# The second block's last convolution channel tile: diagonal f32 matmuls on TensorE in place of taps on VectorE, ScalarE and GpSimd

## The chip, the cores and the metric

The kernel runs on one core of one Trainium2 chip. The metric is the device time of one launch in microseconds: 1757.15 us, median of three runs (1757.03 to 1757.19).

## The reference, cut to what matters

Two transformer blocks follow each other over 512 tokens with model width 1024, all in float32. The second block has, beside an RWKV-7 recurrence of 8 heads, a convolution branch of 512 channels: a gated input, a causal depthwise convolution of 31 taps, a LayerNorm over the channels, and SiLU.

```python
def conformer_conv(u, conv_w, conv_b, ln_g, ln_b):
    h = u[..., :D_CONV] * jax.nn.sigmoid(u[..., D_CONV:])
    h = lax.conv_general_dilated(
        h, conv_w[:, None, :], window_strides=(1,), padding=[(CONV_WIDTH - 1, 0)],
        dimension_numbers=("NWC", "WIO", "NWC"), feature_group_count=D_CONV) + conv_b
    h = layer_norm(h, ln_g, ln_b)
    return jax.nn.silu(h)
...
    y_conv = conformer_conv(p[..., :2 * D_CONV], ...)
    y_rwkv, v_first = rwkv7_mix(p[..., 2 * D_CONV:], ...)
    y = jnp.concatenate([y_conv, y_rwkv], axis=-1) @ w_out[i]
```

Depthwise means that channel c of the result is the sum over the 31 taps of conv_w[tap, c] times channel c of the input, shifted by the tap. Both branches must be there before the product with w_out.

## The kernel before, in words

Activations lie with channels on the 128 partitions and the 512 tokens along the free dimension, so the 512 convolution channels are four tiles, ZC[0] to ZC[3], each 128x542 with 30 leading zeros. A tap of a tile is one pass over 128x512 elements of it at offset `tap`, scaled by a column of weights.

One function, `schedule()`, writes down a single list of steps for all engines, and each engine then emits its own part of every step in that order (`run`). All engines are in-order: an instruction that waits holds back what stands behind it on its engine. Background work is held in Python generators; each call of `pl.step` lets every generator put a few steps. Generators stand in the order conv (`cv1`), conv on GpSimd (`cv2`), `prep` (gates, scan and scaling of a pair of heads `hp`), four `head` generators (the inverse of the recurrence of a head, in levels of 64x64 matmuls), `fin` (states and outputs of a pair). The last projection tile of the block marks `pdone`, and from there `pl.drain()` runs the generators in rounds. I call these rounds R1, R2 and so on. In a round the convolution generators put two steps (weight 2) and each of the others one. A head's round alternates between `x` (a mask product, its transposition, and one more product) and `z` (an update), and every such product is evicted from PSUM by VectorE or ScalarE before the next round's matmuls can start.

The four tiles are shared out like this:
- Tiles 1 and 2: 31 taps each on VectorE (`tap_v`), accumulating in a PSUM bank (`conv.acc`).
- Tile 0: for taps 1 to 30 ScalarE multiplies into one of two buffers, F(45) and F(46) (`tap_g` of ScalarE), and GpSimd adds that to the sum (`tap_g` of GpSimd). ScalarE waits before tap t until GpSimd has done tap t - 2.
- Tile 3: taps 5 to 30 (CSH = 26 of them) in the same ScalarE and GpSimd way into CP = F(58), taps 0 to 4 on VectorE after tile 2, and `conv.join` adds the two parts.

GpSimd reaches tile 3 while the projection tiles 11 to 13 are still running (its first instruction for it is at 976.95 us of the trace) and adds its last tap in R11. VectorE's taps of tile 2 fill two places in each of R1 to R13, with R1's pair at 999.23 us, and tile 3's five taps stand in R14 (two), R15 (two) and R16 (one, with the join after it). The statistics and the norm of the convolution follow from R17 on. `bg_out`, the product of the convolution branch with w_out, starts in R23.

PSUM has 8 banks. In the rounds 6 are in pool M, handed out first in, first out; a step that takes a bank makes TensorE wait until the former user of that bank has been evicted. Through R1 to R13 `conv.acc` of tile 2 holds one of the 6, so 5 go round; in R14 to R16 `conv.acc` of tile 3 holds one.

In each round the steps stand in this order: the convolution's taps, then prep's step for pair hp, then the heads' steps, then fin's. R3 holds `prep.kn` of pair 2, R4 its `prep.vmm`, R6 its `prep.scale`, R7 its `prep.shift`, R8 its `prep.turn`; R11, R12, R13, R14 and R15 hold the scan, `prep.norm`, `prep.kn`, `prep.vmm` with `prep.scale`, and `prep.shift` of pair 3. A pair's chain ends at R10 to R12 with `fin.mu` (R9), `fin.var`, `fin.rs`, `fin.g`.

All matmuls go through the helper `Eng.mm` (line 153), ScalarE copies through `Eng.cp` (L162) and `Eng.act` (L159), elementwise VectorE and GpSimd operations through `Eng.tt` (L165), `Eng.ts` (L169/L170) and `Eng.stt` (L173). So the rows of the profile show helper lines, and an operation is told by its form. One f32 `mm` call leaves two MATMUL instructions in the trace; a call on the float32r operands of the dense layers leaves one.

Of the kernel before, what the change touches and what calls it, by code (L numbers as in the profile page):

```python
# [8 lines left out]
CSH = 26  # L9
LAST = {1: 30, 2: 30, 3: 30 - CSH}  # L10
# [168 lines left out]
class Plan:  # L179
# [13 lines left out]
    def put(self, *step):  # L193
        self.steps.append(step)
# [19 lines left out]
    def has(self, *keys):  # L214
        return all(k in self.done for k in keys)
# [90 lines left out]
def schedule():  # L306
# [242 lines left out]
    def bg_conv_pool():  # L549
        yield from taps(0, 0, 31, "g")  # L550
        yield from taps(3, 31 - CSH, 31, "g")
        mark("cp")

    def bg_conv():
        for i in range(1, 4):
            while not has(("hc", i)):
                yield
            pl.take("M", "conv.acc", i)
            for tap in range(LAST[i] + 1):
                while tap == LAST[i] and i > 1 and not has(("pdone",)):  # L560
                    yield
                put("tap.v", i, tap)
                yield
            pl.rel("M", "conv.acc", i)
        while not has(("cp",)):
            yield
        put("conv.join")
        yield
        pl.take("M", "conv.mean")
        put("conv.mean")  # L570
        pl.rel("M", "conv.mean")
        yield
        for i in range(4):
            put("conv.sq", i)
            yield
        pl.cols("conv.n", "M")
        yield
        pl.spread("conv.n", "M")
        yield
        for i in range(5):  # L580
            if i < 4:
                put("conv.scale", i)
            if i > 0:
                put("conv.out", i - 1)
            yield
        mark("conv")

    cv1, cv2 = bg_conv(), bg_conv_pool()
    pl.begin(cv1, cv2)
    pl.pace[cv1], pl.pace[cv2] = 4, 3  # L590
    pl.weight[cv1], pl.weight[cv2] = 2, 2
# [399 lines left out]
def program(nc, wstream, vecs, cf, cu, xT, metaT, memT, pmix, gup, wau, gupg, out, x2s, kvs):  # L991
# [5 lines left out]
    with ctx:  # L997
# [90 lines left out]
        def freed(*key):  # L1088
            k = pl.before[key]
            if k and k[0] in ("fin.y1", "fin.yc"):  # L1090
                return k[0:2]
            if k and k[0] in DIRECT:
                return DIRECT[k[0]]
            if k and k[0] == "xr.t":
                return ("xr.s", k[1][0:2], 7, 1)
            return k
# [41 lines left out]
        CO, CP = [F(i) for i in CS], F(58)  # L1138
# [163 lines left out]
        def tensor(e):  # L1302
# [171 lines left out]

            def conv_mean():
# [220 lines left out]
            def att_out(g, d):  # L1696
# [10 lines left out]
                "gla.state": gla_state, "gla.out": gla_out, "mix": mix, "conv.mean": conv_mean,  # L1707
# [10 lines left out]
        def scalar(e):  # L1718
# [158 lines left out]
            def tap_g(i, tap, t0):  # L1877
                if tap > t0:
                    wc = vcol("conv_w_2") + tap * 4 + i
                    before = ("conv.g", i, tap - 2) if tap - 2 > t0 else ("conv.g", 0, 30 - tap % 2) if i else None  # L1880
                    e.wait_ge(("mid.hc", i), before)
                    e.cp(F(45 + tap % 2), ZC[i][:, tap:tap + 512], scale=V[:, wc:wc + 1]).then_inc(*e.up("conv.m", i, tap))

# [168 lines left out]
            def evh_dn(i, h):  # L2052
# [8 lines left out]
                "ev.f1": ev_f1, "ev.f2": ev_f2, "ev.cv": ev_cv, "tap.g": tap_g, "conv.sq": conv_sq,  # L2061
# [10 lines left out]
        def vector(e):  # L2072
# [229 lines left out]
            def conv_join():  # L2302
                e.wait_ge(("conv.acc", 3), ("conv.g", 3, 30))
                e.tt(CO[3], CO[3], CP, ADD).then_inc(*e.up("conv.j"))
# [286 lines left out]
        def gpsimd(e):  # L2591
# [53 lines left out]
            def tap_g(i, tap, t0):  # L2645
                dst = CP if i else CO[0]
                c = vcol("conv_w_2") + tap * 4 + i
                if tap == t0:
                    src, w_ = ZC[i][:, tap:tap + 512], V[:, c:c + 1]
                    e.wait_ge(("mid.hc", i))  # L2650
                    if i:
                        e.ts(dst, src, w_, MUL).then_inc(*e.up("conv.g", i, tap))
                    else:
                        e.ts(dst, src, w_, MUL, s2=vec("conv_b_2", i), o2=ADD).then_inc(*e.up("conv.g", i, tap))
# [245 lines left out]
```

## Time and profile before

| what | value |
|---|---|
| median of 3 runs | 1757.15 us |
| the profiled execution's own time | 1757.04 us |
| its span, first to last instruction | 1755.1 us |
| mean granted TensorE clock | 0.968 |
| PE busy | 1661.0 us (95%) |
| VectorE (DVE) busy | 838.8 us (48%) |
| ScalarE (ACT) busy | 606.0 us (35%) |
| GpSimd (POOL) busy | 389.4 us (22%) |

The table is over the whole span. The rounds of the second block's recurrence, roughly 997 to 1140 us, look different from the rest: there TensorE has gaps, its granted clock drops at times, and VectorE is nearly always busy. Times in the rows are microseconds from the span's start. PE is TensorE's matmul side, PEld its weight loads. In a timeline the bracket behind a row is the idle time of that engine before it and the engine and line that ended it.

### The profile page before, as it was taken

How to read it: one execution, taken by the hardware profiler on the slowest of the kernel's cores; microseconds unless marked ns; L12 is line 12 of the kernel's file. 1: busy time of each engine (PE TensorE's matmuls, PEld its weight loads, DVE VectorE, ACT ScalarE, POOL GpSimd, SP SyncE). 2: the span in 40 equal slices, each digit the busy share in tenths (PEclk: the TensorE clock that was granted, in tenths of full speed). 3: DMA queues.
4: the chain of work that ended last, by engine and by line, in shares of the span. 5: the costliest groups of instructions: out<-in, count | busy, mean ns of one | idle time of the engine just before them, and what ended most of it. 6: DMA issues, size and time to landing. Idle time of an engine off the chain costs nothing.

```text
span 1755.1 us, 26846 instructions
## 1 busy us (share of the span) xinstructions
PE 1661.0 (95%) x11510; PEld 1365.6 (78%) x11510; DVE 838.8 (48%) x1256; ACT 606.0 (35%) x973; POOL 389.4 (22%) x333
## 2 busy tenths in 40 slices
PE   6999999999999999999998877898999999999997
PEld 5789878787888888888776666777878878888876
DVE  3377642435433333344756887645642632333334
ACT  4143432324323232243335442334334432222222
POOL 2112111212201011133034540103102341131133
PEclk8899999999999999999999889999999999999999
DMA  5123421224222223222411100013211222223222
GB/s 195 61 84 121 145 73 49 76 87 150 97 96 94 98 76 108 80 96 84 144 50 49 49 3 3 3 50 108 109 41 56 97 88 105 75 94 103 89 78 66
DMA packets 29829, 146.03 MB, mean 83 GB/s; under 512 B 4096, under 2 KB 7440, under 8 KB 14608
## 3 DMA queue, kind: packets, MB, share of 16 engines
q1 hardware_dynamic: 29712, 144.33, 23.4%
q8 instruction: 91, 1.49, 0.4%
q14 instruction: 26, 0.21, 0.0%
HBM read 138.03 MB, written 6.29 MB: 82 GB/s over the span
## 4 chain that ended last, share of the span: by engine, by line
PE 77%; DVE 8%; issue 7%; POOL 4%; ACT 3%; DMA 1%; POOLq 0%; SPq 0%; DVEq 0%; ACTq 0%
PE ps L153 76%; POOL zf L165 3%; DVE zf L165 3%; DVE zf L173 2%; DVE wl L165 1%; DVE ps L173 1%; ACT zf L159 1%; ACT zf L162 1%; ACT wh L162 1%; DMA raw<-in_wstream 1%; ACT zr L162 1%; POOL tn L165 1%; PE ps L156 1%; DVE zf L2344 0%; DVE zr L173 0%
## 5 line engine op out<-in xcount | busy, mean ns | idle before, releaser
L153 PE MATMUL ps<-zr,wh 128*128 128x512 f32 (+1 forms) x3936 | 1173.7, 383 | 16.2 <-DVE wl L165 9.9
L153 PEld LDWEIGHTS ps<-zr,wh 128*128 128x128 f32 x3936 | 716.6, 190 | 175.2 <-DVE wl L165 9.8
L153 PE MATMUL ps<-zr,wl 128*128 128x512 f32 (+1 forms) x1968 | 745.7, 379 | 0.0
L165 POOL TENSOR_TENSOR zf<-zf 128x512 f32<-128x512 f32 (+1 forms) x237 | 283.5, 1203 | 856.4 <-ACT zf L159 587.5
L153 PEld LDWEIGHTS ps<-zr,wl 128*128 128x128 f32 x1968 | 374.0, 190 | 77.1 <-issue 0.8
L165 DVE TENSOR_TENSOR wl<-raw,wh 128x1024 fp32r<-128x1024 f32 (+1 forms) x243 | 306.2, 1300 | 230.5 <-ACT wh L162 230.3
L162 ACT ACTIVATE wh<-raw 128x1024 fp32r<-128x1024 f32 (+1 forms) x243 | 240.4, 1038 | 213.6 <-PE ps L153 211.8
L159 ACT ACTIVATE zf<-zf 128x512 f32<-128x512 f32 (+2 forms) x232 | 127.5, 561 | 396.3 <-DVE zf L165 282.2
L153 PE MATMUL ps<-zf 64*64 64x64 f32 (+6 forms) x3640 | 203.3, 248 | 32.3 <-DVE zf L165 18.1
L153 PEld LDWEIGHTS ps<-zf 64*64 64x64 f32 (+3 forms) x3640 | 162.7, 150 | 72.7 <-issue 31.1
L165 DVE TENSOR_TENSOR zf<-ps,zf 128x512 f32<-128x512 f32 (+2 forms) x165 | 97.6, 597 | 202.8 <-PE ps L153 176.0
L162 ACT ACTIVATE zf<-ps 128x512 f32<-128x512 f32 (+2 forms) x160 | 74.3, 483 | 185.3 <-PE ps L153 169.9
L165 POOL TENSOR_TENSOR zr<-zf,zr 128x512 fp32r<-128x512 f32 x54 | 70.1, 1300 | 280.3 <-ACT zr L162 280.3
L165 DVE TENSOR_TENSOR zf<-zf,ps 128x512 f32<-128x512 f32 (+1 forms) x112 | 62.6, 570 | 140.8 <-PE ps L153 139.7
L162 ACT ACTIVATE zr<-zf 128x512 fp32r<-128x512 f32 x74 | 46.5, 632 | 168.2 <-POOL zf L165 140.0
L153 PE MATMUL ps<-cf_sb,zf 64*64 64x64 f32 (+2 forms) x988 | 64.0, 237 | 24.4 <-ACT zf L159 11.6
L153 PEld LDWEIGHTS ps<-cf_sb,zf 64*64 64x64 f32 (+1 forms) x988 | 59.7, 159 | 28.9 <-POOL zf L165 10.2
L165 POOL TENSOR_TENSOR tn<-tn,cf_sb 128x2 f32<-128x2 f32 (+3 forms) x29 | 31.5, 1089 | 207.3 <-DVE tn L169 115.4
L173 DVE SCALAR_TENSOR_TENSOR zf<-ps,zf 128x512 f32<-128x512 f32 x46 | 31.4, 690 | 92.6 <-PE ps L153 88.6
L162 ACT ACTIVATE zf<-zf,vecs_sb 128x512 f32<-128x512 f32 x73 | 49.7, 716 | 44.2 <-DVE zf L165 36.5
L173 DVE SCALAR_TENSOR_TENSOR ps<-zf,vecs_sb,ps 128x512 f32<-128x512 f32 (+1 forms) x93 | 61.2, 658 | 5.0 <-PE ps L153 3.9
L173 DVE SCALAR_TENSOR_TENSOR zr<-zf,vecs_sb,zr 128x256 fp32r<-128x256 f32 (+1 forms) x64 | 43.8, 696 | 33.0 <-ACT zr L162 33.0
(94 smaller groups left out, 713.1 us busy)
## 6 DMA issues: line engine op xcount, KB each, us to landing
raw<-in_wstream SPq DMA_DIRECT2D x117, 1024.0 KB, 4.8
zf<-in_xT SPq DMA_DIRECT2D x16, 256.0 KB, 3.1
raw<-in_wstream SPq DMA_DIRECT2D x4, 768.0 KB, 4.3
kv_scratch<-zf SPq DMA_DIRECT2D x8, 256.0 KB, 2.2
x_scratch<-zf SPq DMA_DIRECT2D x8, 256.0 KB, 2.1
zf<-x_scratch SPq DMA_DIRECT2D x8, 256.0 KB, 4.4
out<-zf SPq DMA_DIRECT2D x16, 128.0 KB, 1.7
zf<-in_cu SPq DMA_DIRECT2D x1, 1256.0 KB, 10.1
```

The source lines that it names most:

```text
L153: return self.raw.matmul(out_, l, x, start=start, stop=stop)
L156: return self.raw.transpose(out_, in_, idn)
L159: return self.raw.activation(out_, in_, fn, bias=bias, scale=scale)
L162: return self.raw.activation(out_, in_, mybir.ActivationFunctionType.Copy, scale=scale)
L165: return self.raw.tensor_tensor(out_, a, b, o)
L173: return self.raw.scalar_tensor_tensor(out=out_, in0=a, scalar=s, in1=b, op0=o1, op1=o2)
```

## The change

Tile 3 leaves VectorE, ScalarE's multiplications and GpSimd. For each of its 31 taps ScalarE scales the 128x128 identity by the tap's weight column into one of four buffers (CD, which lie in F(58), the former CP), and TensorE multiplies that diagonal matrix with ZC[3] at the tap's offset, 128x128 by 128x512 in f32, accumulating all 31 in one PSUM bank, `conv.p`. A third generator puts these steps two in each round from R1 on (R1 to R15 two, R16 one), before prep, heads and fin. It takes the bank in R1 and gives it back with the join. ScalarE's build of tap t waits for the matmul of tap t - 4. `conv.join` becomes one VectorE operation: PSUM plus the bias into CO[3]. GpSimd keeps tile 0, and the wait that let its second tile follow its first is gone. The join moves from the second place of R16 to the first of R17 and `conv.mean` stays in R17.

```diff
@@ -6,8 +6,7 @@
 P = 128
 UNIT = 2048
 DECAY = math.exp(-0.5)
-CSH = 26
-LAST = {1: 30, 2: 30, 3: 30 - CSH}
+LAST = {1: 30, 2: 30}
 PFIRST = 3
 LAG = 1
 
@@ -548,11 +547,19 @@
 
     def bg_conv_pool():
         yield from taps(0, 0, 31, "g")
-        yield from taps(3, 31 - CSH, 31, "g")
         mark("cp")
 
+    def bg_conv_pe():
+        while not has(("hc", 3), ("pdone",)):
+            yield
+        pl.take("M", "conv.p")
+        for tap in range(31):
+            put("tap.p", tap)
+            yield
+        mark("cpe")
+
     def bg_conv():
-        for i in range(1, 4):
+        for i in range(1, 3):
             while not has(("hc", i)):
                 yield
             pl.take("M", "conv.acc", i)
@@ -562,9 +569,10 @@
                 put("tap.v", i, tap)
                 yield
             pl.rel("M", "conv.acc", i)
-        while not has(("cp",)):
+        while not has(("cp",), ("cpe",)):
             yield
         put("conv.join")
+        pl.rel("M", "conv.p")
         yield
         pl.take("M", "conv.mean")
         put("conv.mean")
@@ -585,10 +593,11 @@
             yield
         mark("conv")
 
-    cv1, cv2 = bg_conv(), bg_conv_pool()
-    pl.begin(cv1, cv2)
+    cv1, cv2, cv3 = bg_conv(), bg_conv_pool(), bg_conv_pe()
+    pl.begin(cv1, cv2, cv3)
     pl.pace[cv1], pl.pace[cv2] = 4, 3
-    pl.weight[cv1], pl.weight[cv2] = 2, 2
+    for g in (cv1, cv2, cv3):
+        pl.weight[g] = 2
     pl.rate = 2
 
     def lag():
@@ -1091,6 +1100,8 @@
                 return k[0:2]
             if k and k[0] in DIRECT:
                 return DIRECT[k[0]]
+            if k and k[0] == "conv.p":
+                return ("conv.j",)
             if k and k[0] == "xr.t":
                 return ("xr.s", k[1][0:2], 7, 1)
             return k
@@ -1135,7 +1146,9 @@
         SC = [F(62 + z) for z in range(4)]
         ZC = [ZF[:, 47 * 512 + 542 * i:47 * 512 + 542 * (i + 1)] for i in range(4)]
         CS = [64, 44, 22, 23]
-        CO, CP = [F(i) for i in CS], F(58)
+        CO = [F(i) for i in CS]
+
+        CD = [F(58)[:, 128 * i:128 * i + 128] for i in range(4)]
         ZB = [F(42), F(43)]
         wau_sb, gupg_sb = F(40), F(41)
         km_ap = [F(47 + i // 2)[:, (i % 2) * 256:(i % 2) * 256 + 256] for i in range(8)]
@@ -1472,6 +1485,11 @@
                 e.wait_ge(freed("in.mx", g), ("in.pool", g), ("in.pm",))
                 e.mm(ps("in.mx", g)[:, :], pmx[:, g * 128:(g + 1) * 128], F(43 + g)).then_inc(*e.up("mm", "in.mx", g))
 
+            def tap_p(tap):
+                e.wait_ge(freed("conv.p") if tap == 0 else None, ("mid.hc", 3), ("conv.d", tap))
+                e.mm(ps("conv.p")[:, :], CD[tap % 4], ZC[3][:, tap:tap + 512], start=(tap == 0),
+                     stop=(tap == 30)).then_inc(*e.up("mm", "conv.p", tap))
+
             def conv_mean():
                 b = ps("conv.mean")
                 e.wait_ge(freed("conv.mean"), ("conv.g", 0, 30), ("conv.acc", 1), ("conv.acc", 2), ("conv.j",))
@@ -1704,7 +1722,7 @@
             run(e, {
                 "mm": mm, "mmm": mmm, "kt": kt, "ko": ko, "mh": mh, "koh": koh, "rows": rows, "cols": cols, "spread": spread, "gla.gate": gla_gate,
                 "gla.score": gla_score, "gla.turn": gla_turn, "gla.turnm": gla_turnm, "gla.state0": gla_state0,
-                "gla.state": gla_state, "gla.out": gla_out, "mix": mix, "conv.mean": conv_mean,
+                "gla.state": gla_state, "gla.out": gla_out, "mix": mix, "tap.p": tap_p, "conv.mean": conv_mean,
                 "prep.gates": prep_gates, "prep.norm": prep_norm, "prep.kn": prep_kn, "prep.vmm": prep_vmm,
                 "prep.turn": prep_turn, "head.a": head_a, "head.pk": head_pk, "head.rt": head_rt, "head.qt": head_qt,
                 "head.ta": head_ta, "head.tz": head_tz, "head.x": head_x, "head.z": head_z, "head.px": head_px,
@@ -1877,9 +1895,13 @@
             def tap_g(i, tap, t0):
                 if tap > t0:
                     wc = vcol("conv_w_2") + tap * 4 + i
-                    before = ("conv.g", i, tap - 2) if tap - 2 > t0 else ("conv.g", 0, 30 - tap % 2) if i else None
-                    e.wait_ge(("mid.hc", i), before)
+                    e.wait_ge(("mid.hc", i), ("conv.g", i, tap - 2) if tap - 2 > t0 else None)
                     e.cp(F(45 + tap % 2), ZC[i][:, tap:tap + 512], scale=V[:, wc:wc + 1]).then_inc(*e.up("conv.m", i, tap))
+
+            def tap_p(tap):
+                c = vcol("conv_w_2") + tap * 4 + 3
+                e.wait_ge(("mm", "conv.p", tap - 4) if tap >= 4 else ("ffn.h", 31))
+                e.cp(CD[tap % 4], ident, scale=V[:, c:c + 1]).then_inc(*e.up("conv.d", tap))
 
             def conv_sq(i):
                 e.wait_ge(("conv.mean",) if i == 3 else ("conv.mt", i))
@@ -2058,7 +2080,7 @@
                 "gla.log": gla_log, "gla.exp": gla_exp, "gla.ends": gla_ends, "gla.turn": gla_turn,
                 "gla.turnm": gla_turnm, "gla.state0": gla_state0, "gla.out": gla_out, "gla.sq": gla_sq, "mix": mix,
                 "ev.po": ev_po, "ev.r": ev_r, "ev.ga": ev_ga, "ev.gb": ev_gb, "og": og, "ev.go": ev_go, "ev.wo": ev_wo,
-                "ev.f1": ev_f1, "ev.f2": ev_f2, "ev.cv": ev_cv, "tap.g": tap_g, "conv.sq": conv_sq,
+                "ev.f1": ev_f1, "ev.f2": ev_f2, "ev.cv": ev_cv, "tap.g": tap_g, "tap.p": tap_p, "conv.sq": conv_sq,
                 "conv.scale": conv_scale, "ev.p": ev_p, "p.mix": p_mix, "prep.gates": prep_gates,
                 "prep.decay": prep_decay, "prep.kk": prep_kk, "prep.v": prep_v, "prep.scale": prep_scale, "prep.shift": prep_shift,
                 "prep.turn": prep_turn, "head.ta": head_ta, "head.tz": head_tz, "head.px": head_px, "head.gh": head_gh,
@@ -2300,8 +2322,8 @@
                     e.stt(CO[i], src, w_, acc, MUL, ADD).then_inc(*e.up("conv.acc", i))
 
             def conv_join():
-                e.wait_ge(("conv.acc", 3), ("conv.g", 3, 30))
-                e.tt(CO[3], CO[3], CP, ADD).then_inc(*e.up("conv.j"))
+                e.wait_ge(("mm", "conv.p", 30), ("mm", "t.p", 13))
+                e.ts(CO[3], ps("conv.p")[:, :], vec("conv_b_2", 3), ADD).then_inc(*e.up("conv.j"))
 
             def conv_mean():
                 e.wait_ge(("mm", "conv.mean"))
@@ -2643,15 +2665,12 @@
                 power(tn_of("mid.b"), ("mid.b3",), "mid.b2")
 
             def tap_g(i, tap, t0):
-                dst = CP if i else CO[0]
+                dst = CO[0]
                 c = vcol("conv_w_2") + tap * 4 + i
                 if tap == t0:
                     src, w_ = ZC[i][:, tap:tap + 512], V[:, c:c + 1]
                     e.wait_ge(("mid.hc", i))
-                    if i:
-                        e.ts(dst, src, w_, MUL).then_inc(*e.up("conv.g", i, tap))
-                    else:
-                        e.ts(dst, src, w_, MUL, s2=vec("conv_b_2", i), o2=ADD).then_inc(*e.up("conv.g", i, tap))
+                    e.ts(dst, src, w_, MUL, s2=vec("conv_b_2", i), o2=ADD).then_inc(*e.up("conv.g", i, tap))
                 else:
                     e.wait_ge(("conv.m", i, tap), ("conv.g", i, tap - 1))
                     e.tt(dst, dst, F(45 + tap % 2), ADD).then_inc(*e.up("conv.g", i, tap))
```

## Rows read from the trace of the kernel before

**Rows 1.** The page: shares of the chain that ended last, over the whole span.
```profile
PE 77%; DVE 8%; issue 7%; POOL 4%; ACT 3%; DMA 1%; POOLq 0%; SPq 0%; DVEq 0%; ACTq 0%
```

**Rows 2.** Busy time by stretch: per engine us and (instructions), then PEclk, DMA share, GB/s.
```profile
997.20:1011.10 13.90, 9.61 (x164) 9.29 (x165) 12.12 (x24) 5.43 (x10) 8.61 (x7) 0.51 0.01 2
...
1031.60:1038.40 6.80, 2.87 (x54) 2.90 (x56) 6.25 (x9) 0.74 (x2) 2.76 (x2) 0.50 0.02 4
...
1069.20:1092.00 22.80, 18.18 (x486) 16.66 (x488) 16.23 (x34) 5.71 (x13) 0.00 (x0) 0.85 0.01 3
```

**Rows 3.** Timeline of TensorE in the rounds: the rows behind its gaps.
```profile
997.22 2.83 PE L153 MATMUL ps<-zf 64*64 64x64 f32 x60 [2.66 <-ACT zf L159]
1004.32 1.54 PE L153 MATMUL ps<-zf 64*64 64x64 f32 x24 [4.26 <-DVE zf L165]
...
1020.32 1.12 PE L153 MATMUL ps<-zf,cf_sb 128*128 128x512 f32 x2 [3.41 <-DVE zf L165]
...
1035.53 1.12 PE L153 MATMUL ps<-zf 64*64 64x64 f32 x16 [7.02 <-DVE zf L165]
...
1048.18 1.12 PE L153 MATMUL ps<-zf,cf_sb 128*128 128x512 f32 x2 [0.93 <-DVE zf L165]
...
1059.54 0.68 PE L153 MATMUL ps<-cf_sb,zf 64*64 64x64 f32 x16 [1.78 <-DVE zf L165]
...
1069.33 1.97 PE L153 MATMUL ps<-cf_sb,tn 128*64 128x128 f32 x16 [3.30 <-POOL tn L165]
...
1085.71 2.65 PE L153 MATMUL ps<-zf 64*64 64x64 f32 x83 [2.86 <-DVE zf L165]
```

**Rows 4.** Timeline of VectorE in the rounds.
```profile
997.54 1.76 DVE L173 SCALAR_TENSOR_TENSOR zf<-zf,vecs_sb 128x511 f32<-128x511 f32 x1
...
1000.67 2.25 DVE L2344 TENSOR_TENSOR_SCAN zf<-cu_sb,zf 128x512 f32<-128x512 uint8 x1
...
1004.30 0.88 DVE L165 TENSOR_TENSOR zf<-zf,cu_sb 128x256 f32<-128x256 f32 x2
...
1018.29 1.64 DVE L173 SCALAR_TENSOR_TENSOR zf<-zf,vecs_sb 128x512 f32<-128x512 f32 x1
...
1029.96 3.42 DVE L173 SCALAR_TENSOR_TENSOR zf<-zf 128x512 f32<-128x512 f32 x2
1033.42 1.63 DVE L165 TENSOR_TENSOR zf<-zf 128x512 f32<-128x512 f32 x1
...
1056.93 1.22 DVE L2344 TENSOR_TENSOR_SCAN zf<-cu_sb,zf 128x512 f32<-128x512 uint8 x1
...
1073.19 0.75 DVE L173 SCALAR_TENSOR_TENSOR zf<-zf,vecs_sb 128x512 f32<-128x512 f32 x1
...
1083.09 1.41 DVE L173 SCALAR_TENSOR_TENSOR zf<-zf 128x512 f32<-128x512 f32 x2
1084.54 0.69 DVE L165 TENSOR_TENSOR zf<-zf 128x512 f32<-128x512 f32 x1
...
1087.85 1.54 DVE L173 SCALAR_TENSOR_TENSOR ps<-zf,vecs_sb,ps 128x512 f32<-128x512 f32 x2
```

**Rows 5.** Timeline of ScalarE just before R1.
```profile
993.32 1.94 ACT L162 ACTIVATE zf<-zf,vecs_sb 128x512 f32<-128x512 f32 x3
995.87 0.72 ACT L162 ACTIVATE zf<-zf,vecs_sb 128x512 f32<-128x512 f32 x1 [0.61 <-POOL zf L165]
996.50 1.25 ACT L159 ACTIVATE zf<-ps,vecs_sb 128x512 f32<-128x512 f32 x2
```

**Rows 6.** Groups of GpSimd, 976 to 1048 us: busy us, mean ns, idle before.
```profile
L165 POOL TENSOR_TENSOR zf<-zf 128x512 f32<-128x512 f32 x26 | 36.4, 1400 | 31.4 <-ACT zf L162 28.8
```

**Rows 7.** Timeline of TensorE: the four f32 calls of the convolution's mean.
```profile
1095.15 3.70 PE L153 MATMUL ps<-zf,cf_sb 128*128 128x512 f32 x8
```

**Rows 8.** Groups of ScalarE, 990 to 1100 us.
```profile
L162 ACT ACTIVATE zf<-zf,vecs_sb 128x512 f32<-128x512 f32 x27 | 18.5, 717 | 6.8 <-POOL zf L165 3.6 <-DVE zf L165 3.0
...
L159 ACT ACTIVATE dsm<-dsm 128x8 f32<-128x8 f32 x2 | 0.4, 208 | 8.6 <-DVE dsm L165 8.6
```

## The prediction, made before the changed kernel ran

> **What bounds the kernel now.** I read the chain of waits first. Over the span TensorE holds 77% of it [rows 1], so most of the kernel is dense matmuls that this change does not touch. The change lies in R1 to R16, from 997.2 to about 1092 us, and there the picture is another one. By stretches [rows 2] TensorE is busy 9.61 of the first 13.90 us and VectorE 12.12; between 1031.6 and 1038.4 TensorE has 2.87 of 6.80 and VectorE 6.25. The third thing to see in those rows is the clock: 0.51 and 0.50 in two of the stretches and 0.85 in the third, so TensorE spends part of this stage at 1.2 GHz, and each time it had been idle before.
>
> The timeline of TensorE [rows 3] then gives each gap and who ended it: 2.66 us for ScalarE, 4.26, 3.41, 7.02, 1.78 and 2.86 us for VectorE, 3.30 us for GpSimd's power that stands between `prep.norm` and `prep.kn` of pair 3. So the rounds are a ring of TensorE and VectorE. A round is as long as its matmuls plus the evictions behind them, and where prep has much elementwise work, VectorE alone sets it. The taps of the convolution are filler in this ring, but filler that stands ahead of the heads' steps in every queue.
>
> **The change, part by part.** I sum against the profiled execution's 1757.04 us (span 1755.1, 1.94 us outside it), which is 0.11 us under the median of the runs.
>
> *ScalarE's hold before R1 goes.* ScalarE does three tap products (1.94 us), waits 0.61 us for GpSimd's sum, does a fourth (0.72), and only then the two tanh of the gates of pair 2 at 996.50 [rows 5]. TensorE waits for these: 2.66 us [rows 3]. The products and the wait, 3.27 us, are gone before the tanh (the diagonals are not put until R1), so the whole gap closes: -2.7.
>
> *VectorE stops being slowed by GpSimd.* GpSimd's adds for tile 3 take most of the 36.4 us of [rows 6], and they lie on 976.95 to 1047 us. In that time some VectorE operations take far longer than the same form later, when GpSimd is idle [rows 4]: the scan of prep 2.25 against 1.22; the STT of two SBUF tiles 1.64 against 0.75; two of them in `prep.scale` 3.42 against 1.41, and the multiplication after them 1.63 against 0.69; and the mix of the last projection tile 1.76, against which I set the 0.75 of the STT one element longer. A tap into PSUM (1.54 the pair) has that price in R15, with GpSimd idle, and in the rounds before as well. What I expect: 1.01 and 1.03 in R1, 0.89 twice in R3 (the second such operation of `prep.kn` stands right before the one shown, alike), 2.01 and 0.94 in R6. In R1 not all of this is won, see the bank below. R3 -1.8, R6 -2.95. The other end is 0, if the stretching has another cause.
>
> *VectorE loses five taps and the join changes form.* Five at 0.75 to 0.8. The two of R15 (1.54) and the one of R16 (0.75) stand between a state update and `prep.shift` or the last masks, with TensorE waiting: -2.2 of 2.3. The pair of R14 stands beside TensorE's transposition of v and costs nothing. The join is one 128x512 operation in both kernels: 0.
>
> *TensorE gets 31 f32 matmuls.* Before, the four f32 calls of the mean, the same shape and accumulating in one bank, took 3.70 us [rows 7], 0.925 each. 31 make 28.7 us, 1.85 in each of R1 to R15. The Trainium skill ("FP8 and Floating Point Precision", TensorE Precision Notes) counts four passes for true f32; at 2.4 GHz that is 0.85 us for 512 columns and 26.5 us for 31, an estimate; the row is 8% above it and is what I use. What of it lies on the path, by round:
> - R1: the pair runs while VectorE is still at scan and masks (gap of 4.26): 0.
> - R2: TensorE is done with the small `prep.norm` matmuls 1.4 us before VectorE has done its own taps: 0.4. R4: the gap of 3.41 shrinks by R3's 1.8 to 1.6, so 1.85 leaves 0.2.
> - R6 and R7: the gap of 7.02 less 2.95 is 4.1, and two pairs are 3.7: 0. R12 and R13: the gap of 3.30 and the time until VectorE reads `prep.norm`: 0. R15: the gap of 2.86: 0.
> - R3, R5, R8, R9, R10, R11, R14 and half of R16: nothing but small gaps stands there, so 7.5 pairs, 13.9 us, less the gaps of 0.93 and 1.78: 11.2.
>
> Together +11.8. The bounds: 0, if all is hidden, and 28.7, if none is (at the low clock twice that again for the pairs that meet it).
>
> *ScalarE's 31 diagonals.* 128x128 with a weight column is not in the trace. Below is the 128x8 activation, 208 ns, above the 128x512 of the same form, 717 ns [rows 8]. The size is nearer to the small one, so I take 300 ns: 0.6 a round, where two tap products of 0.7 were until R10. The builds stand behind ScalarE's evictions of the round before, which TensorE's heads need anyway. Cost 0. If it doesn't hold, see the fourth case.
>
> *One bank less.* In R1 to R13 `conv.p` and `conv.acc` both hold banks, so 4 go round in place of 5. In R1 the last `fin.n` product takes the bank of the second head's mask and not of the first's. That is evicted one product, one addition and one mask later: 0.88 us for the first two [rows 4] and near half of that for the mask, 1.3, its place being the gap of 4.26. It eats that much of the 2.04 of R1 and leaves -0.7. In R9 `fin.mu` waits for one eviction more in the same way (its gap of 0.93 is for this): +1.2. Elsewhere the evictions are ahead. In R14 to R16 nothing changes, as `conv.acc` of tile 3 is not taken. Bounds 0 and 5 (0.4 more in the x rounds too).
>
> *The clock.* About 22 us of matmul work in the rounds runs at 1.2 GHz (9.6, 2.9 and, from the third stretch's 0.85, near 6.8 [rows 2], the rest around 1022). At 2.4 GHz it would take 11 us less. The spells come with the gaps, and the taps and the quicker VectorE fill most of those; but some of that work is evictions rather than columns, and R1 keeps a gap. I take half: -5.5, between 0 and -11. The Trainium skill ("TensorE: Matmul & The Clock Gate", What's actually happening) has activity release the throttle. By that rule, with the gaps of R4, R7, R13 and R15 filled, nearly all spells vanish, which is the second case.
>
> *The tail.* The join comes one place later, but `conv.mean` stays in R17, and by counting places `bg_out` still starts in R23: 0.
>
> Sum: -2.7 -0.7 -1.8 -2.95 -2.2 +11.8 +1.2 -5.5 = -2.85. ScalarE's evictions in the x rounds also find a shorter queue (0.6 in place of 1.4 us [rows 8]); I give that 0.5, so -3.35. 1757.0 - 3.3 = 1753.7.
>
> **The rivals.**
> 1. *Likeliest, 0.45*: as summed, 1753.7, own range 1751 to 1756.5.
> 2. *The clock holds, 0.20*: the full 11 us in place of 5.5, 1748.2. For it: every low stretch has a gap in or before it. Against it: R1's gap stays, and a spell may just move.
> 3. *The clock gives nothing, 0.20*: the spells move with the stage, 1753.7 + 5.5 = 1759.2. For it: even the stretch from 1069 us, with GpSimd idle, has 0.85. Against it: 28.7 us of wide matmuls are the strongest filling there is.
> 4. *The diagonals come late, 0.15*: TensorE's pair waits behind ScalarE's evictions of the round before and then for the build, an eviction of 0.4 and two builds of 0.6, so 1.0 in each of 7.5 bare rounds, +7.5: 1761.2, slower than before. Place: TensorE's wait for ScalarE ahead of the first tap of a round. It decides as soon as ScalarE reaches the builds later than TensorE ends the last round. For it: the buffers are built in the round of their use, not ahead. Against it: in the z rounds ScalarE has nothing to evict, and it is the least busy of the three.
>
> **How the numbers follow.** About 3.5 us, 0.2%, is what a measurement of this kernel can tell from no change. Faster by more, under 1753.6: half of case 1 and all of case 2, and a little of 3: 0.46. Within: the rest of case 1, most of 3, a third of 4: 0.38. Slower, over 1760.7: the rest of 4, and case 3 where the bank costs its upper bound: 0.16. The range goes from 1746.5 (case 2 with a little more of the taps hidden) to 1761.5 (just past case 4).
>
> **What would show it.** GpSimd idle from about 975 us to the powers of pair 2, no 2.66 us gap before R1, the scan of pair 2 at 1.2 us and `prep.scale`'s pair at 1.4: the gains in R1 to R6. TensorE's tap pair 1.85 us apart in the timeline, the gaps at R4, R7, R13 and R15 nearly closed, PEclk above 0.85 from 997 to 1092: the filling and the clock. R16's end earlier by 3 to 4 us than before, then the same lengths until the end. It would be wrong if TensorE waits for ScalarE's diagonals, if the VectorE operations stay long with GpSimd idle, or if R8 to R11 grow by more than 1.85 each.

## The result, and the profile after

Slower. The median is 1774.63 us (1773.36 to 1787.05, four runs) against 1757.17 us for the kernel before on the same chip, +17.5 us; the ratio is 1.0114, 95% interval 1.0069 to 1.0159. The forecast of 1753.7 us is missed by 21 us and its range by 13. The profiled execution took 1774.54 us (span 1772.6).

The kernels share their frame up to the rounds, and `conv.mean`, where the change ends, comes 17.0 us later (1095.15 in [rows 7], 1112.11 now). So all of the loss lies between R1 and there. In the page the chain that ended last is nearly what it was [rows 1]:

```profile
PE 78%; DVE 8%; issue 7%; POOL 4%; ACT 3%; DMA 1%; POOLq 0%; SPq 0%; DVEq 0%; ACTq 0%
```

Shares of the whole span cannot show this loss, since 17 us in 1770 are 1%. I use two stretches, cut where the work is the same in every kernel: from VectorE's tap pair of R1 to that of R13 (R1 to R12), and from there to `conv.mean` (R13 to R17). Columns as in [rows 2]: window, its length, then busy us and (instructions) of PE, PEld, DVE, ACT and POOL, PEclk, DMA share, GB/s. Before:

```profile
999.23:1068.71 69.48, 48.51 (x1138) 43.39 (x1134) 58.68 (x113) 27.46 (x55) 29.04 (x21) 0.84 0.01 2
1068.71:1095.15 26.44, 21.32 (x547) 19.50 (x547) 18.82 (x40) 7.67 (x17) 0.48 (x1) 0.87 0.01 3
```

The kernel after, the same two, and R2 alone:

```profile
996.75:1078.38 81.63, 70.36 (x1262) 49.95 (x1262) 53.83 (x114) 24.15 (x62) 4.93 (x3) 0.96 0.01 2
1078.38:1112.11 33.73, 26.12 (x560) 19.18 (x559) 16.14 (x36) 9.33 (x22) 0.00 (x0) 0.95 0.01 2
1004.16:1013.54 9.38, 9.04 (x208) 6.83 (x206) 3.48 (x10) 1.84 (x6) 1.65 (x1) 0.80 0.01 2
```

R1 to R12 grew by 12.2 us and R13 to R17 by 7.3, although VectorE has less to do and the clock rose from 0.84 and 0.87 to 0.96 and 0.95. Outside TensorE's busy time there are 18.9 us in place of 26.1. (Some records of small matmuls are missing from the trace of the kernel before: R1 to R12 show 1138 there, and 1262 less the 48 of the taps, so 1214, in the kernel after. So the kernel before has somewhat more busy time and less idle time than these figures say; the lengths of the stretches don't depend on it.)

What the change was meant to do to the other engines did happen. ScalarE just before R1, which answers to [rows 5]: the tap products are gone, the gates' evictions come 2.1 us earlier, and two diagonals stand behind them. (One product of the same form is left, at 993.76. The kernel without tile 3's products has it too, at 993.54, so it is no tap, and one of the four that the prediction counted in [rows 5] was never part of the hold.)

```profile
993.76 0.72 ACT L161 ACTIVATE zf<-zf,vecs_sb 128x512 f32<-128x512 f32 x1 [1.37 <-DVE zf L164]
994.39 1.25 ACT L158 ACTIVATE zf<-ps,vecs_sb 128x512 f32<-128x512 f32 x2
995.53 0.69 ACT L161 ACTIVATE zf<-cf_sb,vecs_sb 128x128 f32<-128x128 f32 x2
```

The operations of VectorE in [rows 4] that were long have their short durations, 0.74 for 1.76, 1.22 for 2.25, 0.75 for 1.64, 1.41 for 3.42, 0.69 for 1.63:

```profile
995.75 0.42 DVE L169 TENSOR_SCALAR zf<-zf 128x512 f32<-128x512 f32 x1
996.09 0.74 DVE L172 SCALAR_TENSOR_TENSOR zf<-zf,vecs_sb 128x511 f32<-128x511 f32 x1
...
998.20 1.22 DVE L2366 TENSOR_TENSOR_SCAN zf<-cu_sb,zf 128x512 f32<-128x512 uint8 x1
...
1019.14 0.75 DVE L172 SCALAR_TENSOR_TENSOR zf<-zf,vecs_sb 128x512 f32<-128x512 f32 x1
...
1032.42 1.41 DVE L172 SCALAR_TENSOR_TENSOR zf<-zf 128x512 f32<-128x512 f32 x2
1033.87 0.69 DVE L164 TENSOR_TENSOR zf<-zf 128x512 f32<-128x512 f32 x1
```

The first of these rows is VectorE's first operation behind ScalarE's gates. In the kernel before it was

```profile
997.20 0.43 DVE L170 TENSOR_SCALAR zf<-zf 128x512 f32<-128x512 f32 x1 [1.03 <-ACT zf L159]
```

so it comes 1.45 us earlier now, and the mix behind it (0.74 for 1.76) adds 1.0 us before VectorE's tap pair of R1.

On GpSimd, 976 to 1048 us, the 36.4 us of [rows 6] have become one addition:

```profile
L164 POOL TENSOR_TENSOR zf<-zf 128x512 f32<-128x512 f32 x1 | 1.6, 1554 | 0.1
```

TensorE's timeline shows where new time stands; its gaps answer to [rows 3], the last row to [rows 7]:

```profile
996.07 3.33 PE L152 MATMUL ps<-zf 128*128 128x512 f32 x64 [2.41 <-ACT zf L161]
1000.81 6.51 PE L152 MATMUL ps<-zf 64*64 64x64 f32 x60 [1.42 <-DVE zf L164]
...
1014.23 1.99 PE L152 MATMUL ps<-zf 128*128 128x512 f32 x4 [0.93 <-ACT zf L161]
...
1054.61 3.59 PE L152 MATMUL ps<-zf 128*128 128x512 f32 x21 [1.47 <-ACT zf L161]
...
1112.11 3.67 PE L152 MATMUL ps<-zf,cf_sb 128*128 128x512 f32 x8 [1.35 <-DVE zf L168]
```

The gap before R1 is still there (2.41 for 2.66): the first tap pair waits for its diagonals. The gap of 4.26 in R1 is 1.42. A pair of taps takes 1.99 us. In the waits of TensorE from 994 to 1092 us (us in all, times, longest) ScalarE's copies, the diagonals among them (L161), stand first, and VectorE's 21.9 us are 6.5:

```profile
PE ps L152 <- ACT zf L161: 8.8, 7, 2.4
PE ps L152 <- DVE zf L164: 6.5, 6, 2.0
```

ScalarE's 31 builds cost 394 ns each, against which [rows 8] had 717 for a product and 208 for a small activation (group over 990 to 1115 us: busy, mean ns, idle before):

```profile
L161 ACT ACTIVATE zf<-cf_sb,vecs_sb 128x128 f32<-128x128 f32 x31 | 10.5, 394 | 0.0
```

L161 is the helper of all copies; where diagonals are built early (an experiment below), 0.8 us of such waits remain, so about 8 of the 8.8 are the diagonals'. Read alone, these rows say that rival 4 came true. The experiments show that this is not where the 17.5 us went.

### The profile page after: what moved, and what is told of

It is laid out like the page before. It is cut to its first block, busy times and chain, and to the rows that moved or that the text cites. A ratio compares the mean times of both kernels' runs of the same rounds, so it can differ in the third digit from the quotient of the medians.

```text
span 1772.6 us, 26915 instructions
## 1 busy us (share of the span) xinstructions
PE 1685.6 (95%) x11572; PEld 1370.5 (77%) x11572; DVE 829.3 (47%) x1251; ACT 599.6 (34%) x979; POOL 353.9 (20%) x307
## 4 chain that ended last, share of the span: by engine, by line
PE 78%; DVE 8%; issue 7%; POOL 4%; ACT 3%; DMA 1%; POOLq 0%; SPq 0%; DVEq 0%; ACTq 0%
PE ps L152 77%; POOL zf L164 3%; DVE zf L164 2%; DVE zf L172 2%; DVE wl L164 1%; DVE ps L172 1%; ACT zf L161 1%; ACT zf L158 1%; DMA raw<-in_wstream 1%; ACT wh L161 1%; ACT zr L161 1%; POOL tn L164 1%; PE ps L155 0%; DVE zf L2366 0%; POOL zr L164 0%
## 5 line engine op out<-in xcount | busy, mean ns | idle before, releaser
L164 POOL TENSOR_TENSOR zf<-zf 128x512 f32<-128x512 f32 (+1 forms) x212 | 249.7, 1184 | 833.6 <-ACT zf L158 598.7
L161 ACT ACTIVATE wh<-raw 128x1024 fp32r<-128x1024 f32 (+1 forms) x243 | 240.4, 1038 | 213.0 <-PE ps L152 210.5
L152 PE MATMUL ps<-zf 64*64 64x64 f32 (+6 forms) x3702 | 231.7, 250 | 29.4 <-ACT zf L161 14.9
L152 PEld LDWEIGHTS ps<-zf 64*64 64x64 f32 (+3 forms) x3702 | 169.0, 146 | 86.2 <-issue 43.7
L161 ACT ACTIVATE zf<-ps 128x512 f32<-128x512 f32 (+2 forms) x160 | 74.5, 484 | 214.8 <-PE ps L152 189.2
L161 ACT ACTIVATE zr<-zf 128x512 fp32r<-128x512 f32 x74 | 46.5, 632 | 167.4 <-POOL zf L164 140.1
L164 DVE TENSOR_TENSOR zf<-zf 128x512 f32<-128x512 f32 (+4 forms) x74 | 50.7, 699 | 11.1 <-ACT zf L158 10.7
```

Of the source, the lines that this page charges most:

```text
L152: return self.raw.matmul(out_, l, x, start=start, stop=stop)
L161: return self.raw.activation(out_, in_, mybir.ActivationFunctionType.Copy, scale=scale)
L164: return self.raw.tensor_tensor(out_, a, b, o)
```

## The experiments

Each number is a median less the median of the kernel before, measured beside it on the same chip, then the ratio with its 95% interval (0.001 of the ratio is 1.8 us). Kernels from different sections ran on different chips, so their differences to the kernel before are compared, and a difference of 1 or 2 us between two of them is not resolved. "Early" means that a diagonal is built a round before its use.

### The gains alone

The kernel before without the taps of tile 3 that ScalarE and GpSimd make (taps 5 to 30 are left out). VectorE's five and the bank of their sum stay, nothing is given to TensorE.

```
-        yield from taps(3, 31 - CSH, 31, "g")
...
-                e.wait_ge(("conv.acc", 3), ("conv.g", 3, 30))
-                e.tt(CO[3], CO[3], CP, ADD)
+                e.wait_ge(("conv.acc", 3))
+                e.ts(CO[3], CO[3], 1.0, MUL)
```

> The kernel before with tile 3's taps 5 to 30 left out on ScalarE and GpSimd (their sum is not added; taps 0 to 4 stay on VectorE). It measures the gain side of the change alone. Theory A (the gains came as predicted, the matmuls and ScalarE's diagonals cost more than they): 8 to 11 us under the kernel before, about 1747. Rival B (the gains of R1 and R6 are given back later, since the rounds hang on other waits): within 3 us of the kernel before, 1754 to 1757.

Measured: 1750.33, -7.9 us; 0.9948 (0.9933 to 0.9963). The two stretches of its trace:

```profile
996.53:1060.62 64.09, 48.79 (x1132) 43.52 (x1128) 52.39 (x113) 17.16 (x38) 4.45 (x3) 0.84 0.01 3
1060.62:1086.28 25.66, 19.58 (x546) 17.90 (x546) 18.64 (x39) 7.66 (x17) 0.48 (x1) 0.93 0.01 4
```

R1 starts 2.7 us earlier, R3 lasts 5.47 us in place of 7.30 and R6 4.95 in place of 7.92; R11 gives 1.0 back (11.37 for 10.38). Here, where no diagonal stands in the way, TensorE's gap before R1 is 0.55 us:

```profile
994.89 1.90 PE L153 MATMUL ps<-zf 64*64 64x64 f32 x60 [0.55 <-ACT zf L159]
```

The side of the gains was sized nearly right (7.9 us, just under the 8 to 11 expected). From here on the question is what costs 25 us, not 17.5.

### The matmuls taken out, and the change repeated

From the changed kernel, taps 1 to 29 have no matmul (29 of 31 taps are left out of tile 3); all 31 diagonals are built, each behind the one four before it, and the bank is held. Beside it the changed kernel again, unedited.

```
             def tap_p(tap):
+                if 0 < tap < 30:
+                    return
```

> The changed kernel with the matmuls of taps 1 to 29 left out; taps 0 and 30 stay, all 31 diagonals are built, the bank is held. Theory A (TensorE's own time is most of the loss): 1750 to 1755. Rival C (ScalarE's queue and the bank): over 1760.

> The changed kernel once more, unchanged, so that the other three have it on the same chip. 1773 to 1776 under every theory.

Measured: without matmuls 1760.70, +2.7 us; 1.0016 (1.0006 to 1.0026). The change again 1775.76, +17.8; 1.0107 (1.0090 to 1.0123). So the 29 matmuls are worth 15.1 us of their 26.8, and what is left is still 10.6 us above the kernel with the gains alone. The 15.1 are a net value: without the matmuls TensorE's clock is lower (0.81 in R1 to R12, which last 72.53 us, against 0.96 and 81.63 with them). The 10.6 are the bank, or diagonals that almost nothing waits for; the next runs part these.

### The diagonals early, or not built

First: `tap.d` for taps 0 and 1 before R1, then for tap t + 2 behind tap t. Second: matmuls with the identity in place of the diagonals and no build on ScalarE (all 31 weights of tile 3 are left out).

```
+            put("tap.d", 0)
+            put("tap.d", 1)
...
             put("tap.p", tap)
+            if tap + 2 < 31:
+                put("tap.d", tap + 2)
```
```
-                e.mm(ps("conv.p")[:, :], CD[tap % 4], ZC[3]...
+                e.mm(ps("conv.p")[:, :], ident, ZC[3]...
```

> The changed kernel with each diagonal built one round ahead: taps 0 and 1 before R1, tap t + 2 right behind the step of tap t. TensorE waited 9.6 us in all for ScalarE ahead of these matmuls. Theory D (late diagonals are a cost of their own): 7 to 10 us under the changed kernel, about 1766. Rival A2 (the wait only stands in the place of the one for VectorE or for the state update that ends the round before): under 3 us of gain, 1772 or more.

> The changed kernel with the identity in place of all 31 diagonals and ScalarE's builds left out (the sum is then unweighted). The matmuls are the same in number and form. Under theory D it goes as the kernel with early diagonals or 1 to 2 us below it, 1764 to 1766, and what is left over e1's time is TensorE's matmuls and the bank. Under rival A2 it stays at 1771 or more.

Measured: early 1769.96, +11.8; 1.0061 (1.0046 to 1.0076). Identity 1769.44, +11.2; 1.0060 (1.0041 to 1.0079). So the building itself costs nothing that can be seen if it is early enough, and lateness costs about 6 of the 17.8 us with this number of banks. That lies between the two expectations (7 to 10 us, or under 3). Two thirds of the loss are something else.

### The bank

`conv.p` from D, a pool that stands idle in the rounds, in place of M, from which the heads' steps take theirs; once with early diagonals and once as the only edit of the changed kernel.

```
-        pl.take("M", "conv.p")
+        pl.take("D", "conv.p")
...
-        pl.rel("M", "conv.p")
+        pl.rel("D", "conv.p")
```

> The kernel with early diagonals (e3_early), with the bank for the sum taken from pool D, whose two banks lie idle in R1 to R16, so 5 go round in pool M as before the change. Theory E (the missing bank costs 2 to 5 us): 1765 to 1768. Rival (it costs nothing, evictions are ahead): within 1 us of e3_early's 1770.

> The changed kernel with the sum's bank from pool D and nothing else: diagonals are built late as in the changed kernel. If bank and late diagonals add, it is 4 to 6 us above the kernel with both mended (1763.9), so 1768 to 1770. If they are one and the same wait (a late diagonal is only late because the ring of 4 banks is), it is within 2 us of 1764.

Measured: early with the bank of D 1763.85, +5.9; 1.0039 (1.0024 to 1.0054). The bank alone 1763.27, +4.9; 1.0028 (1.0019 to 1.0038). Two changed words give back 12.9 us of 17.8, and with them early diagonals bring nothing more: the bank is worth more than the 2 to 5 us expected, and the two mends don't add. Stretches of the bank alone, and its R2:

```profile
996.59:1071.53 74.94, 66.41 (x1262) 47.45 (x1262) 53.40 (x114) 23.92 (x62) 4.93 (x3) 1.00 0.01 2
1071.53:1101.06 29.53, 24.40 (x560) 18.80 (x559) 15.96 (x36) 9.44 (x22) 0.00 (x0) 1.00 0.01 2
1004.01:1009.97 5.96, 5.48 (x205) 5.18 (x203) 3.29 (x11) 1.86 (x6) 1.65 (x1) 1.00 0.01 3
```

Half of the 6.7 us that R1 to R12 lose to the bank is R2, 9.38 against 5.96 us. The number of instructions is nearly the same (208 and 205); the clock is 1.00 in place of 0.80. The low spell starts in R1, whose clock is 0.79 in the change and 1.00 here: by windows of 1 us it stands at 0.50 from 1001 to 1007 us and at 0.59 in the next, near 7 us in all. At half the clock this loses an estimated 3.4 us, and as VectorE sets the length of R1 (7.41 and 7.42 us), it shows in R2. What TensorE did before it, here:

```profile
995.91 4.09 PE L152 MATMUL ps<-zf 128*128 128x512 f32 x96 [2.40 <-ACT zf L161]
1000.66 0.92 PE L152 MATMUL ps<-zf 64*64 64x64 f32 x24 [0.66 <-DVE zf L164]
```

The gap of 0.66 was 1.42 in the change. It ends at the same moment of R1 (4.1 us after VectorE's tap pair starts, in both), but with the bank 32 more matmuls fit ahead of it. From R3 to R12 the clock is 1.00 in both kernels, so the other 3.3 us of R1 to R12 (1.3 in R4, 1.0 in R10, 0.5 each in R7 and R11) are not the clock. The kernel with early diagonals shows the same thing from the other side. Its R1 pair is done sooner, so a longer gap stands behind it:

```profile
1000.81 5.26 PE L152 MATMUL ps<-zf 64*64 64x64 f32 x28 [3.11 <-DVE zf L164]
```

and then R2 takes 9.64 us at 0.64, though it has the bank:

```profile
1004.16:1013.80 9.64, 9.64 (x208) 8.51 (x207) 3.47 (x11) 1.86 (x6) 1.65 (x1) 0.64 0.01 3
```

That is why "early" brought nothing here: what it won in R10 and R12 (7.68 and 2.85 us against 9.41 and 4.88) it lost in R2. In the kernel with late diagonals both rounds hold a wait for them; R12's is

```profile
1066.36 1.98 PE L152 MATMUL ps<-zf 128*128 128x512 f32 x4 [2.33 <-ACT zf L161]
```

The counterpart: the kernel before, from which one bank of M is taken at R1, left empty, and given back at the join.

```
+    def bg_hold():
+        while not has(("hc", 3), ("pdone",)):
+            yield
+        held.append(pl.pools["M"].pop(0))
...
         put("conv.join")
+        pl.pools["M"].append(held.pop())
```

> The kernel before with one more bank of pool M held idle from R1 to the join, so that 4 go round in R1 to R13 and 4 in R14 to R16; nothing else differs. Theory E (the bank alone is a main cost, 5 to 10 us): 1763 to 1768. Rival (my step's +1.2 and 1.3, by eviction order): 1758 to 1761.

Measured: 1771.88, +13.5; 1.0066 (1.0048 to 1.0084), by which it would be 11.6; more than the 5 to 10 expected. No tap matmul and no diagonal is in it. Its stretches:

```profile
1001.00:1081.45 80.45, 57.30 (x1154) 49.66 (x1154) 58.77 (x114) 27.79 (x55) 29.00 (x21) 0.73 0.01 2
1081.45:1109.06 27.61, 21.18 (x546) 19.22 (x546) 18.91 (x39) 7.77 (x17) 0.48 (x1) 0.88 0.01 3
```

R1 to R12 last 11.0 us longer than before. 8.8 of it is TensorE's busy time, for nearly the same instructions (1154 records and 1138), at 0.73 in place of 0.84; only 2.2 are more idle time. The largest part is R10, 9.86 us at 0.68 in place of 5.85 at 1.00. `fin.mu` shows how it begins: at the end of R9 three short gaps follow each other, and then the matmuls that took 1.12 us in [rows 3] take 2.08:

```profile
1055.18 0.68 PE L153 MATMUL ps<-zf 64*64 64x64 f32 x16 [0.88 <-DVE zf L165]
1056.43 0.68 PE L153 MATMUL ps<-cf_sb,zf 64*64 64x64 f32 x16 [0.57 <-DVE zf L165]
1057.69 2.08 PE L153 MATMUL ps<-zf,cf_sb 128*128 128x512 f32 x2 [0.57 <-DVE zf L165]
```

### Filling by gap, and fewer matmuls

24 taps on TensorE in the rounds where it has gaps (4, 0, 0, 2, 1, 2, 3, 0, 1, 0, 2, 1, 3, 1, 3, 1 in R1 to R16), seven on GpSimd after tile 0; bank of D, diagonals early.

```
+PLACE = [4, 0, 0, 2, 1, 2, 3, 0, 1, 0, 2, 1, 3, 1, 3, 1]
+NP = 24
...
+        for r, n in enumerate(PLACE):
+            for _ in range(n):
+                put("tap.p", tap)
+                tap += 1
...
+        yield from taps(3, NP, 31, "g")
...
-                e.ts(CO[3], ps("conv.p")[:, :], vec("conv_b_2", 3), ADD)
+                e.stt(CO[3], ps("conv.p")[:, :], vec("conv_b_2", 3), CP, ADD, ADD)
```

> 24 taps on TensorE, put by round where the kernel before has a gap (4, 0, 0, 2, 1, 2, 3, 0, 1, 0, 2, 1, 3, 1, 3, 1 in R1 to R16), diagonals built one round ahead, the bank from pool D; the last 7 taps on GpSimd right behind tile 0, before R1. Theory A (a pair of matmuls costs its full time where there is no gap and nothing in one): 1751 to 1755, faster than the kernel before. Rival F (the matmuls cost wherever they stand, since one delay in a ring is carried on): 1762 or more.

Measured: 1753.88, -4.1; 0.9977 (0.9968 to 0.9986), faster than before. Two edits of it: the same 24 taps two a round (`PLACE = [2]*12 + [0]*4`), and the bank from M.

> The kernel with 24 taps on TensorE and 7 on GpSimd, the 24 put two in each of R1 to R12 in place of by gap; buffers, bank and early diagonals as there. Theory A (where a matmul stands decides what it costs): 4 to 8 us over the one placed by gap (1753.9), 1758 to 1762. Rival (the number alone decides): within 1.5 us of 1753.9.

> The kernel placed by gap with the sum's bank from pool M, as in the changed kernel. Theory E: 3 to 6 us over 1753.9, 1757 to 1760. Rival (with fewer matmuls in the crowded rounds the bank no longer matters): within 1.5 us of 1753.9.

Measured: even 1757.57, -0.8; 0.9990 (0.9981 to 1.0000). With the bank of M 1763.49, +5.1; 1.0026 (1.0016 to 1.0036): here the bank is worth 9.2 us, where 3 to 6 were expected. Placing the 24 taps is worth 3.3 by the medians and 2.3 by the ratios, whose intervals overlap, so with 24 taps the gain of the placing is not clear of the noise, and it is below the 4 to 8 expected.

All 31 taps on TensorE by gap, with `PLACE = [4, 1, 1, 2, 2, 3, 4, 1, 1, 1, 2, 1, 3, 1, 3, 1]`:

> All 31 taps on TensorE, GpSimd with tile 0 only, as in the changed kernel, but the sum's bank from pool D, diagonals one round ahead, and the taps put by gap (4, 1, 1, 2, 2, 3, 4, 1, 1, 1, 2, 1, 3, 1, 3, 1) in place of two a round. Theory A: 4 to 7 us under the even placing with the same bank (1763.9), 1757 to 1760. Rival: within 2 us of it.

Measured: 1754.88, -4.3; 0.9980 (0.9968 to 0.9993). Two a round with all else alike had +5.9, so the same 31 matmuls cost 10 us less where the gaps are, more than the 4 to 7 expected and far outside both intervals. Its stretches:

```profile
995.54:1062.18 66.64, 63.84 (x1259) 46.94 (x1258) 52.82 (x114) 23.93 (x60) 4.45 (x3) 1.00 0.01 3
1062.18:1090.42 28.24, 23.77 (x560) 18.55 (x558) 16.05 (x36) 9.17 (x21) 0.48 (x1) 1.00 0.01 3
```

TensorE is idle for 2.8 us in twelve rounds. That is the state on which the prediction counted for the changed kernel.

### One bank more

If a bank fewer costs this much, D's second idle bank may be worth something in the rounds. It is lent to M from R1 to the start of the products with w_out; in the kernel before, and in the mix of 24 and 7.

```
     pl.pools["M"].append(pl.pools["D"].pop(0))
+    pl.pools["M"].append(pl.pools["D"].pop(0))
     pl.begin(bg_out())
...
+        pl.pools["D"].append(pl.pools["M"].pop(0))
         for uu in range(2):
```

> The kernel before with the second idle bank of pool D lent to pool M from R1 to the start of the w_out products, so one bank more goes round (6 in R1 to R13 in place of 5). Theory E (the rounds hang on the number of banks): 3 to 8 us faster than before, 1750 to 1755. Rival (5 were enough, and only the step to 4 hurts): within 2 us of before.

> The kernel with 24 taps placed by gap and 7 on GpSimd, with the same lending of the second bank of pool D. Theory E: 3 to 6 us under 1753.9, 1748 to 1751. Rival: within 1.5 us of 1753.9.

Measured: the kernel before with it 1755.19, -4.0; 0.9977 (0.9967 to 0.9986). The mix with it 1748.91 (1747.33 to 1750.11), -10.3; 0.9941 (0.9929 to 0.9954). This is the best version found, and faster than both kernels. In the kernel before, five banks to six gain 4 us, five to four lose 13.5 by the medians and 11.6 by the ratio.

## Why the prediction was wrong

The forecast was -3.35 us and the repeated change has +17.8. The runs divide the difference: the gains were to give 10.0 and gave 7.9; the taps, with VectorE's five and the clock, were to cost 4.1 and cost 12.8; the bank was to cost 2.5 and cost 12.9.

**Right: the gains, in part by luck.** In all -7.9 was measured where the sum has 2.7 + 2.04 + 1.8 + 2.95 + 0.5 = 10.0 without bank and taps. In the kernel with the gains alone R3 is shorter by 1.83 (predicted 1.8) and R6 by 2.97 (2.95). R1 starts 2.5 us earlier (predicted 2.7), but not by the reason given: VectorE's first operation behind ScalarE's gates came only 1.45 us earlier, and the other 1.0 is the mix in front of R1's tap pair, which I had counted inside R1. The gap that was to close is 2.41 us in the changed kernel, where the first tap pair waits for its diagonals, and 0.55 without diagonals. R1 itself is 1.0 shorter, with the bank and without; my 2.04 less 1.3 was near that only because two errors cancel. That the neighbours slowed VectorE is confirmed by every row above. The runs take GpSimd's additions and ScalarE's products away together; ScalarE still has 24.15 us of work in R1 to R12 of the changed kernel while these operations are short, which speaks for GpSimd. The Trainium skill ("SBUF — State Buffer", SBUF: two separate sides) has VectorE, with two SBUF inputs, and GpSimd lock each other out of a shared pair of ports for a whole instruction. The rows agree: it is operations on two SBUF tiles that fell (1.64 to 0.75), while a tap into PSUM (1.53 and 1.54 the pair) and the operation on one tile (0.43 and 0.42) kept their time.

**Wrong, the first step that failed: "One bank less", +2.5, bounds 0 and 5.** The changed kernel loses 12.9 us with it, the mix 9.2, and a bank merely held empty costs the kernel before 13.5 (11.6 by the ratio). With early diagonals it is 5.9. The place in R1 was right, but R1 itself is as long with the bank as without (7.42 and 7.41 us), so not the 1.3 that I put there, and R9, where I put 1.2, is 5.10 us in both. Two things were left out. The clock is lower behind such gaps: 3.4 us in R2, a round with almost no idle time to show for it. And I walked along the ring of the kernel before for the two places where a bank is taken late; with four banks R4, R7, R10 and R11 grew as well (1.3, 0.5, 1.0 and 0.5 against the bank of D). For R13 to R17 I said that nothing changes. The bank of D wins 4.2 us there too (33.73 to 29.53), but with it six banks go round there, and before had five, as the change has. Of the trace's 10.9 us between the two, the predicted term answers to the 6.7 of R1 to R12, and for the held bank to 11.0. Both are above my upper bound.

**Wrong, the second: the taps on the path, +11.8.** From the gains alone to the change with D's bank the measured step is +12.8 us. For the same step the sum has 11.8 - 2.2 for VectorE's taps - 5.5 for the clock = 4.1. By trace it is 14.7: 10.9 in R1 to R12 and 3.9 after. By rounds: R3 +2.3, R5 +1.7, R8 +2.5, R10 +3.6, R12 +2.0, R4, R6 and R9 0 to 0.5. So R3, R5 and R8 were named rightly but for the size; R9 (+0.5) and R11 (-1.0) were better. R12 was to be free and R10 was to cost one pair. In both the pair waits for its diagonals, 1.5 us in R10 behind the evictions of `fin.mu` and 2.3 in R12, which is rival 4's mechanism in two places; with early diagonals R12 is free as predicted (2.85 us, 2.84 without taps) and R10 is 7.68. A pair among other matmuls takes 1.98 us and not the 1.85 of the sum, 2.0 us for all 31. In R13 to R17 I had +0.6 (1.5 pairs less the taps of VectorE): measured +3.9 with six banks and +8.1 with the change's five. Part of this was put at nothing in the prediction: the join. It now stands right before `conv.mean`, and TensorE waits 1.35 us for it in every kernel that has the matmuls and 0 in the kernel before; no run moves the join alone.

**One sum would have told.** I hid 28.7 - 11.8 = 16.9 us of matmuls in gaps, closed 9.0 of gaps by the gains and VectorE's taps, and 0.5 for ScalarE, and gave 2.5 back for the bank. Of TensorE's 26.1 idle us in the stretch that leaves some 2. The change has 18.9, with the bank of D 13.7; only the placement by gap came to 7.3. No term alone looked too good; the total did.

**The clock, -5.5.** PEclk did rise above 0.85 as forecast, to 0.96, and 1.00 with D's bank. How much time it gave back I can't part from the rest: no run changes the clock alone. Busy time is a hint. 69.8 us before and 28.7 of matmuls make 98.5; the change has 96.5, the bank of D 90.8, so 2 and 8 us, and rather more, as the 69.8 lack the missing records. The Trainium skill ("TensorE: Matmul & The Clock Gate", What's actually happening) has the throttle as the default state and activity release it. R2 agrees: 0.64 behind a gap of 3.11, 0.80 behind 1.42, 1.00 behind 0.66. By rival 2 this clock meant 1748; it came with 1763 to 1775, so a full clock was not the gain that I took it for.

**Diagonals, 0, and rival 4.** 394 ns each and not 300. TensorE's waits for ScalarE come to 8.8 us up to 1092 us in the change and 9.3 with the bank of D, and the time of the two differs by 13 us. With the bank of D early diagonals bring nothing (1763.85 against 1763.27): what R10 and R12 win, R2 loses to the clock. With the bank of M they bring 6. Named as a rival at 1761.2 with 7.5 us on the path, the wait was seen, but its length is not its price: a TensorE that did not wait there waited elsewhere or ran at a lower clock.

**The tail, 0.** Right: +17.0 at `conv.mean`, +17.5 at the end.

**Open.** How the price of a bank divides between clock and waits is read from one profile each: 8.8 busy and 2.2 idle of 11.0 for the held bank, 4.0 and 2.7 of 6.7 for the change's. Whether the five taps taken from VectorE gave their 2.2 us was not tried alone. The bank's price with early diagonals (5.9) is half of that with late ones (12.9); R2, slow with either bank when the diagonals are early, accounts for 3.4 of the difference; the rest is not traced.

## What to carry to other kernels

A long-lived accumulator takes a bank from a ring: before counting the work that it moves, run the old kernel with one bank held empty, and look for a pool that is idle at the time. Filler on TensorE is paid for by where it stands, so place it by the gaps of each round, and add up all the idle time that a forecast means to hide against what the trace has. A wait that comes first in the list is a cost only if taking it away shortens the run.

## What was unexpected on the chip

- 0.8 us more of a gap in R1, with 32 more small matmuls left behind it, came with 3.4 us more in the next round (0.66 and 1.42 us of gap; 5.96 us at 1.00 and 9.38 at 0.80 for R2).
- One PSUM bank of the ring of five, held empty in the kernel before, costs 11.6 to 13.5 us where the stage is 96 us long; a sixth gains only 4. Most of the price there is busy time at a lower clock (8.8 of 11.0 us in R1 to R12, at 0.73 for 0.84).
- A 128x128 f32 activation from SBUF with a weight column takes 394 ns, a little over half of the 128x512 product's 717.
- At the full clock an f32 128x512 matmul takes 0.99 us in a pair among small ones (1.98 to 1.99 the pair) and 0.92 in a row of four (3.67).
